# Another order of the SBUF allocations in a three-layer fp32 kernel on one core

## The chip, the core and the metric

One core of a Trainium2 chip runs the whole program. The core has five engines with a queue of instructions each: TensorE (PE; its weight loads are shown apart, as PEld), VectorE (DVE), ScalarE (ACT), GpSimd (POOL) and SyncE (SP), which issues the DMAs. The metric is the device time of one execution in microseconds. SBUF is the working memory; an address in it, here and below, is the byte offset within a partition.

## The reference

Two layers of a first block (normalisation, a mixer, normalisation, a feed-forward part with a convolution along the sequence), then one layer of a second block with two kinds of attention and 32 experts. There are 256 tokens of width 1,024, all in fp32. Cut to its frame:

```python
def first_block(x, ...):
    h = x
    for i in range(DEPTH):                       # DEPTH = 2: mla_mixer, then diff_mixer
        a = rms_norm(h, norm_g[i, 0])
        ...
        h = h + rms_norm(a, norm_g[i, 1])
        f = conv_ffn(rms_norm(h, norm_g[i, 2]), ffn_w_up[i], ffn_conv_w[i], ffn_conv_b[i], ffn_w_down[i])
        h = h + rms_norm(f, norm_g[i, 3])
    return h

def hybrid_layer(x, ...):
    h = rms_norm_2(x, g_mix)
    ...
    mixed = jax.nn.sigmoid(ga) * (o_a @ w_proj_a) + jax.nn.sigmoid(gb) * (o_b @ w_proj_b)
    x = x + mixed @ w_out
    x = x + hier_moe(rms_norm_2(x, g_ffn), w_group, b_group, w_expert, b_expert, w1, w3, w2)
    return x

    # in hier_moe, for each expert:
        hid = jax.nn.silu(xb @ w1[e]) * (xb @ w3[e])
        return hid @ w2[e]
```

The feed-forward part has 2,816 hidden columns, each expert 512. Each token goes to two experts.

## The kernel before

**Dense layers, to about 877 us.** Weights come in pieces of up to 128 x 2,048 fp32. SyncE loads a piece into one of four places of raw, ScalarE copies it to fp32r as the high part (L1330), and GpSimd subtracts the two for the low part (L635); both parts lie in parts, four places with a high and a low half each. TensorE multiplies in fp32r, three products for each pair of tiles, high x high, high x low, low x high, at L683, L684 and L685 in the helper product(). The activations are split in the same way: xh and xl, and for the second operand of a feed-forward part hh and hl. There are two forms. by_feature loads 128 columns of weights from parts as the stationary operand and streams 256 tokens of xh or xl past them (256 columns). by_token loads 128 tokens from xh, xl, hh or hl as the stationary operand and streams parts past them (mostly 512 columns). In the profile's names the streamed operand stands ahead of the stationary one: bank<-xh,parts is the 256-column form, bank<-parts,hh the 512-column form. A feed-forward layer has 33 pieces, 22 for the way up and 11 for the way down; pieces 8 to 31 are in a loop that runs twice over 12. keep_clock (L712) repeats a product of xh with itself where TensorE would otherwise pause.

**Attention** works in fp32 on views of room, a scratch buffer of 46,592 bytes for each partition. The probabilities of the second block's attention lie in xn and gpost and are transposed at L1146, with the identity from cs as the streamed operand.

**Experts, from about 877 us.** The experts run in 16 pairs. Each of the six weight matrices of a pair is a DMA of 2 MB into one of eight slots, taken in turn: six slots are the sixths of ring (which lies over raw and parts), one is the end of room, one is xspare (which lies over xh and xl). SyncE issues them at L592 as slots come free. Matmuls at L1258 (w1 and w3) and L1286 (w2) stream the slots at 512 columns past activations in room, two experts side by side in 64 columns of the array each. L1201 gathers the tokens and L1231 adds the result of a pair, from hh and hl with selT as the stationary operand. At the end VectorE adds to h (L2283), GpSimd applies the gains (L658) and the output is stored from xn.

**Where buffers lie.** sb(name, shape) takes the next free address, rounded up to 32 bytes; a buffer opened in a with statement gives its room back at the end of it, which is how ring lies over raw and parts, and xspare over xh and xl. The order of the calls at the head of build() is thus the map of SBUF. All semaphores, queues and the order of work are written out by hand further on in build() and don't look at addresses.

Of the kernel before, what the change touches and what calls it, by code (L numbers as in the profile page):

```python
# [28 lines left out]
F32R = mybir.dt.float32r  # L29
# [5 lines left out]
P = 128  # L35
S = 256
NT = S // P
D = 1024
KT = D // P
# [25 lines left out]
HALF = 2048  # L65
# [159 lines left out]
def build(nc, A, cst, out):  # L225
    G, A_, BANK, TURNS, W = plan()
    ctx = ExitStack()
    with ctx:
        def sb(name, shape, dt=F32):
            return ctx.enter_context(nc.sbuf_tensor(name, shape, dt))  # L230
# [6 lines left out]
        with nc.sbuf_tensor("raw", [P, RING, PIECE], F32) as raw, \  # L237
                nc.sbuf_tensor("parts", [P, PARTS, 2, PIECE], F32R) as both:
            high, low = both[:, :, 0, :], both[:, :, 1, :]
        ring = sb("ring", [P, 3 * RING, HALF])  # L240
        cs = sb("cs", [P, C_END + 5 * P + 16 * FT])
        prow = cs[:, C_END:C_END + 5 * P].rearrange("p (a b) -> p a b", b=P)
        subT = sb("subT", [P, 1])
        convT = cs[:, C_END + 5 * P:].rearrange("p (l w a j) -> p l w a j", l=2, w=4, a=2)
        gpre, gpost = sb("gpre", [P, D]), sb("gpost", [P, D])
        wr = sb("wr", [P, KT, NG + NE])
        br = sb("br", [P, NG + NE])
        lamp = sb("lamp", [P, 4, HD])
        h = sb("h", [P, NT, D])
        xn = sb("xn", [P, NT, D])  # L250
        with nc.sbuf_tensor("xh", [P, KT, S], F32R) as xh, nc.sbuf_tensor("xl", [P, KT, S], F32R) as xl:
            pass
        xspare = sb("xspare", [P, 2 * HALF])
        hh, hl = sb("hh", [P, 4, S], F32R), sb("hl", [P, 4, S], F32R)
        st = sb("st", [P, 64])
        eps_t = sb("eps_t", [P, 9])
        att = sb("att", [P, 4, 2, 2, 2])
        room = sb("room", [P, 11648])

        def view(at, n):  # L260
            return room[:, at:at + n]

        def r3(ap, **k):
            return ap.rearrange("p (a b) -> p a b", **k)
# [31 lines left out]
        qbT, kbT = r3(view(2048, 1024), b=S), r3(view(3072, 1024), b=S)  # L296
        va, vb = r3(view(6144, 1024), b=512), r3(view(7168, 1024), b=512)
        qiT, kiT = qrT, krT
        score = sb("score", [P, NT, S])
        selm = r3(prow[:, 0:4, :].rearrange("p a b -> p (a b)"), b=S)  # L300
        work = [score[:, :, :], selm]
        tanh_of = [view(4096, 2048), view(0, 2048)]
# [8 lines left out]
        silu = view(1536, EF)  # L311
        hidT = r3(view(2048, EF), b=P)
        Sel = view(2560, NT * 2 * CAP).rearrange("p (t e c) -> p t e c", t=NT, e=2)
        selT = sb("selT", [P, 2, NT, P], F32R)
        yh, yl = (y[:, :, :].rearrange("p a b -> p (a b)") for y in (hh, hl))
        gate, posm, mask = (r3(view(10240 + 64 * n, NT * NE), b=NE) for n in range(3))
        lg = r3(view(10432, NT * 36), b=36)
# [2037 lines left out]
```

## Time and profile before

| | us |
|---|---|
| median of three timed runs | 1345.78 |
| lowest and highest of them | 1342.06, 1347.07 |
| the profiled execution | 1344.84 |
| its span, first to last instruction | 1343.0 |

In the span TensorE is busy for 1282.2 us, GpSimd 573.2, ScalarE 548.2 and VectorE 509.6. The mean granted clock of TensorE is 0.994 of 2.4 GHz. The DMA moves 341.22 MB.

A matmul's time in the profile runs from its start to the modelled end of its way through the array, and the next one starts before that end. The pace of a run of products is therefore the distance between starts, which the view in order of time shows, and not the mean duration. Busy times of a group count overlapped time once.

### The profile page before, as it was taken

Reading aid. Unit: us, or ns where it says so; the run is one execution under the profiler, and the core shown is the slowest. Engines: PE = TensorE matmul, PEld = TensorE weight load, DVE = VectorE, ACT = ScalarE, POOL = GpSimd, SP = SyncE. Lnnn points to the kernel's source line nnn. Section 1 sums busy time; section 2 is a strip of 40 time slices with the busy share of each in tenths; the row PEclk is TensorE's granted clock in tenths of the full one; section 3 lists DMA queues with packets and bytes.
Section 4 is the critical chain, followed back from the end, with each engine's and each line's share of the span. In section 5 each row is a group of like instructions: output and inputs, shape, how many; then the busy total and the mean of one; then the engine's idle time right before and its main releaser. Section 6 shows DMA issues by size and latency. Waiting matters only on the chain.

```text
span 1343.0 us, 20033 instructions
## 1 busy us (share of the span) xinstructions
PE 1282.2 (95%) x7959; PEld 953.8 (71%) x7959; DVE 509.6 (38%) x1303; ACT 548.2 (41%) x853; POOL 573.2 (43%) x136
## 2 busy tenths in 40 slices
PE   6998999999998899999999999999999999999996
PEld 6867999998986799999878888854444444454442
DVE  2434444445265454444657453421111111111112
ACT  4654555556477465555543664311111111111112
POOL 4722788885944188888567855200000000000001
PEclk9999999999999999999999999999999999999998
DMA  7731566664633276664446544889999999999994
GB/s 270 235 94 63 184 194 188 188 193 151 220 126 95 63 205 195 196 188 165 150 164 204 158 137 161 335 342 405 427 428 427 429 429 429 429 428 428 428 424 185
DMA packets 157078, 341.22 MB, mean 254 GB/s; under 512 B 8554, under 2 KB 119499, under 8 KB 144331
## 3 DMA queue, kind: packets, MB, share of 16 engines
q1 hardware_dynamic: 157002, 340.18, 68.2%
q8 instruction: 53, 0.87, 0.3%
q14 instruction: 23, 0.18, 0.0%
HBM read 339.10 MB, written 1.05 MB: 253 GB/s over the span
## 4 chain that ended last, share of the span: by engine, by line
PE 77%; DMA 11%; ACT 4%; DVE 4%; POOL 2%; issue 1%; SPq 0%; ACTq 0%; DVEq 0%
PE bank L683 16%; PE bank L685 15%; PE bank L684 15%; PE bank L1258 12%; DMA ring<-in_w 6%; PE bank L1286 6%; DMA xspare<-in_w 4%; PE bank L1201 3%; PE bank L782 2%; POOL parts L635 2%; PE bank L693 1%; PE bank L1231 1%; ACT parts L1330 1%; PE bank L1119 1%; PE bank L1135 1%
## 5 line engine op out<-in xcount | busy, mean ns | idle before, releaser
L635 POOL TENSOR_TENSOR parts<-raw,parts 128x2048 fp32r<-128x2048 f32 (+4 forms) x128 | 568.0, 4464 | 289.8 <-ACT parts L1330 289.8
L683 PE MATMUL bank<-xh,parts 128*128 128x256 f32 x1032 | 288.0, 279 | 5.8 <-POOL parts L635 3.8
L684 PE MATMUL bank<-xl,parts 128*128 128x256 f32 x1032 | 285.8, 277 | 0.0
L685 PE MATMUL bank<-xh,parts 128*128 128x256 f32 x1032 | 285.8, 277 | 0.0
L1330 ACT ACTIVATE parts<-raw 128x2048 fp32r<-128x2048 f32 (+4 forms) x128 | 236.0, 1852 | 23.4 <-PE bank L683 8.5
L1258 PE MATMUL bank<-ring,room 128*64 128x512 f32 x768 | 226.1, 594 | 7.2 <-DMA ring<-in_w 5.3
L658 POOL TENSOR_TENSOR xn<-h,gpost 128x512 f32<-128x512 f32 x4 | 4.9, 1268 | 474.6 <-DVE h L2283 474.6
L683 PEld LDWEIGHTS bank<-xh,parts 128*128 128x128 f32 x1032 | 193.8, 188 | 12.4 <-issue 4.7
L684 PEld LDWEIGHTS bank<-xl,parts 128*128 128x128 f32 x1032 | 194.0, 188 | 0.8
L685 PEld LDWEIGHTS bank<-xh,parts 128*128 128x128 f32 x1032 | 194.0, 188 | 0.0
L1258 PEld LDWEIGHTS bank<-ring,room 128*64 128x64 f32 x768 | 72.6, 137 | 111.7 <-issue 111.7
L683 PE MATMUL bank<-parts,xh 128*128 128x512 f32 (+5 forms) x304 | 114.7, 377 | 5.9 <-DVE xl L1763 2.2
L1286 PE MATMUL bank<-ring,room 128*64 128x512 f32 x384 | 115.0, 600 | 0.7 <-ACT room L1693 0.7
L684 PE MATMUL bank<-parts,xh 128*128 128x512 f32 (+5 forms) x304 | 112.5, 370 | 0.0
L685 PE MATMUL bank<-parts,xl 128*128 128x512 f32 (+5 forms) x304 | 112.2, 369 | 0.0
L1693 ACT ACTIVATE room<-bank 128x512 f32<-128x512 f32 x16 | 9.6, 598 | 194.4 <-PE bank L1272 194.4
L685 PE MATMUL bank<-parts,hl 128*128 128x512 f32 x192 | 75.6, 394 | 0.0
L683 PE MATMUL bank<-parts,hh 128*128 128x512 f32 x192 | 74.8, 389 | 0.8 <-POOL parts L635 0.8
L684 PE MATMUL bank<-parts,hh 128*128 128x512 f32 x192 | 75.3, 392 | 0.0
L1509 ACT ACTIVATE room<-bank,room 128x256 f32<-128x256 f32 x64 | 32.7, 562 | 102.2 <-PE bank L685 101.0
L1367 ACT ACTIVATE room<-bank 128x512 f32<-128x512 f32 (+1 forms) x75 | 41.1, 581 | 75.1 <-PE bank L693 32.5
L1286 PEld LDWEIGHTS bank<-ring,room 128*64 128x64 f32 x384 | 34.9, 138 | 51.5 <-issue 49.3
(256 smaller groups left out, 1858.5 us busy)
## 6 DMA issues: line engine op xcount, KB each, us to landing
ring<-in_w SPq DMA_DIRECT2D x67, 2048.0 KB, 22.6
raw<-in_ffn_w_up SPq DMA_DIRECT2D x88, 512.0 KB, 4.9
raw<-in_ffn_w_down SPq DMA_DIRECT2D x44, 512.0 KB, 3.9
room<-in_w SPq DMA_DIRECT2D x11, 2048.0 KB, 19.9
xspare<-in_w SPq DMA_DIRECT2D x11, 2048.0 KB, 25.6
raw<-in_w_in SPq DMA_DIRECT2D x40, 512.0 KB, 4.0
raw<-in_diff_w_qkv SPq DMA_DIRECT2D x24, 512.0 KB, 4.6
ring<-in_w SPq DMA_DIRECT2D x10, 1024.0 KB, 25.0
```

What stands on the lines that cost most here:

```text
L635: pool.tensor_tensor(low[:, p % PARTS, 0:n], raw[:, p % RING, 0:n], high[:, p % PARTS, 0:n], ALU.subtract).then_inc(low_ready, 1)
L683: first = pe.matmul(out_, a[0], b[0], start=start, stop=False)
L684: pe.matmul(out_, a[0], b[1], start=False, stop=False)
L685: return first, pe.matmul(out_, a[1], b[0], start=False, stop=stop)
L693: ins = pe.transpose(b[0:cols, at:at + rows], src, ident[0:rows, 0:rows])
L782: ins = pe.matmul(b[:, t * S:t * S + S], qs[n][:, t * P:t * P + P], ks[n], start=n == 0, stop=n == len(qs) - 1)
L1201: ins = pe.matmul(bank[2 + k // 4][:, P * (k % 4):P * (k % 4) + P], xn[:, t, P * k:P * k + P], Sel[:, t].rearrange("p e c -> p (e c)"), st ...
L1258: ins = pe.matmul(bank[x][CAP * e:CAP * e + CAP, :], XgT[:, k, CAP * e:CAP * e + CAP], rows, start=k == 0, stop=k == KT - 1)
L1286: ins = pe.matmul(bank[1 + hf][CAP * e:CAP * e + CAP, :], hidT[:, k, CAP * e:CAP * e + CAP], rows_of(j, 2, e, k, D)[:, 512 * hf:512 * hf + ...
L1330: act.activation(high[:, p % PARTS, 0:n], raw[:, p % RING, 0:n], ACT.Copy).then_inc(high_ready, 1)
L1367: act.activation(dst, src, func, scale=scale).then_inc(bank_moved[BANK[g]], 1)
L1509: act.activation(fbuf[b][a], bank[b][:, a * S:a * S + S], ACT.Identity, bias=par(3, a), scale=par(1, a)).then_inc(centre, 1)
```

## The change

The calls that allocate the buffers stand in another order. The buffers that TensorE reads come first, each with a size that is a multiple of 512 bytes; the table of constants cs and the small columns (subT, wr, br, lamp, st, eps_t, att) come after them. Nothing else differs: on each of the five engines the built program has the same instructions in the same order (4,910 rows on PE, counting runs of equal ones once), with other addresses in them.

```diff
         ring = sb("ring", [P, 3 * RING, HALF])
+
+        with nc.sbuf_tensor("xh", [P, KT, S], F32R) as xh, nc.sbuf_tensor("xl", [P, KT, S], F32R) as xl:
+            pass
+        xspare = sb("xspare", [P, 2 * HALF])
+        hh, hl = sb("hh", [P, 4, S], F32R), sb("hl", [P, 4, S], F32R)
+        h = sb("h", [P, NT, D])
+        xn = sb("xn", [P, NT, D])
+        room = sb("room", [P, 11648])
+        gpre, gpost = sb("gpre", [P, D]), sb("gpost", [P, D])
+        score = sb("score", [P, NT, S])
+        selT = sb("selT", [P, 2, NT, P], F32R)
         cs = sb("cs", [P, C_END + 5 * P + 16 * FT])
         prow = cs[:, C_END:C_END + 5 * P].rearrange("p (a b) -> p a b", b=P)
         subT = sb("subT", [P, 1])
         convT = cs[:, C_END + 5 * P:].rearrange("p (l w a j) -> p l w a j", l=2, w=4, a=2)
-        gpre, gpost = sb("gpre", [P, D]), sb("gpost", [P, D])
         wr = sb("wr", [P, KT, NG + NE])
         br = sb("br", [P, NG + NE])
         lamp = sb("lamp", [P, 4, HD])
-        h = sb("h", [P, NT, D])
-        xn = sb("xn", [P, NT, D])
-        with nc.sbuf_tensor("xh", [P, KT, S], F32R) as xh, nc.sbuf_tensor("xl", [P, KT, S], F32R) as xl:
-            pass
-        xspare = sb("xspare", [P, 2 * HALF])
-        hh, hl = sb("hh", [P, 4, S], F32R), sb("hl", [P, 4, S], F32R)
         st = sb("st", [P, 64])
         eps_t = sb("eps_t", [P, 9])
         att = sb("att", [P, 4, 2, 2, 2])
-        room = sb("room", [P, 11648])
...
-        score = sb("score", [P, NT, S])
...
-        selT = sb("selT", [P, 2, NT, P], F32R)
```

The addresses that follow, from the built programs (bytes within a partition; "past" is the remainder after division by 512). The first 16,384 bytes are reserved and a few constants follow them, so that the first buffer starts at 16,512.

| buffer | bytes | before | past | after | past |
|---|---|---|---|---|---|
| raw, ring | 32,768, 98,304 | 16,512 | 128 | 16,512 | 128 |
| parts | 65,536 | 49,280 | 128 | 49,280 | 128 |
| xh, xspare | 8,192, 16,384 | 152,640 | 64 | 114,816 | 128 |
| xl | 8,192 | 160,832 | 64 | 123,008 | 128 |
| hh | 4,096 | 169,024 | 64 | 131,200 | 128 |
| hl | 4,096 | 173,120 | 64 | 135,296 | 128 |
| h | 8,192 | 136,256 | 64 | 139,392 | 128 |
| xn | 8,192 | 144,448 | 64 | 147,584 | 128 |
| room | 46,592 | 177,664 | 0 | 155,776 | 128 |
| gpre | 4,096 | 125,728 | 288 | 202,368 | 128 |
| gpost | 4,096 | 129,824 | 288 | 206,464 | 128 |
| score | 2,048 | 224,256 | 0 | 210,560 | 128 |
| selT | 2,048 | 226,304 | 0 | 212,608 | 128 |
| cs | 10,880 | 114,816 | 128 | 214,656 | 128 |
| wr | 1,152 | 133,920 | 288 | 225,568 | 288 |

## Rows read from the trace of the kernel before

**Rows 1.** The chain that ended last, by engine, and its shares by line.
```profile
PE 77%; DMA 11%; ACT 4%; DVE 4%; POOL 2%; issue 1%; SPq 0%; ACTq 0%; DVEq 0%
...
by line: PE bank L683 15.9%; PE bank L685 15.5%; PE bank L684 15.4%; PE bank L1258 11.7%; DMA ring<-in_w 6.1%; PE bank L1286 5.9%; DMA xspare<-in_w 4.5%; PE bank L1201 3.1%; PE bank L782 1.9%; POOL parts L635 1.5%; PE bank L693 1.4%; issue 
```

**Rows 2.** Stretches: us, each engine's busy us (instructions), PEclk, DMA share, GB/s.
```profile
180.00:304.00 124.00, 124.00 (x923) 117.11 (x923) 55.72 (x134) 66.67 (x82) 103.19 (x24) 1.00 0.64 197
464.00:476.00 12.00, 11.51 (x96) 11.30 (x96) 3.23 (x7) 6.04 (x7) 3.21 (x1) 1.00 0.01 1
...
1130.00:1290.00 160.00, 151.09 (x814) 73.96 (x812) 26.66 (x61) 18.96 (x26) 0.00 (x0) 1.00 1.01 429
```

**Rows 3.** Groups by line and shape, TensorE: count, busy us, mean ns, idle before.
```profile
L683 PE MATMUL bank<-xh,parts 128*128 128x256 f32 x1032 | 288.0, 279 | 5.8 <-POOL parts L635 3.8 <-issue 1.8 <-DVE room L1851 0.2
...
L683 PE MATMUL bank<-parts,xh 128*128 128x512 f32 x216 | 87.5, 405 | 3.2 <-DVE xl L1763 2.2 <-DVE xl L1761 1.0
...
L683 PE MATMUL bank<-parts,hh 128*128 128x512 f32 x192 | 74.8, 389 | 0.8 <-POOL parts L635 0.8
...
L683 PE MATMUL bank<-hh,parts 128*128 128x256 f32 x32 | 9.2, 286 | 0.0
```

**Rows 4.** In order of time, TensorE: start us, duration us, line, tiles, shape.
```profile
135.01 0.28 PE L683 MATMUL bank<-xh,parts 128*128 128x256 f32 x1
...
137.01 0.28 PE L685 MATMUL bank<-xh,parts 128*128 128x256 f32 x1
...
199.73 0.28 PE L685 MATMUL bank<-xh,parts 128*128 128x256 f32 x1
...
205.96 0.28 PE L683 MATMUL bank<-xh,parts 128*128 128x256 f32 x1
...
639.69 0.39 PE L684 MATMUL bank<-parts,hh 128*128 128x512 f32 x1
...
646.79 0.39 PE L685 MATMUL bank<-parts,hl 128*128 128x512 f32 x1
647.02 7.45 PE L712 MATMUL bank<-xh 128*128 128x512 f32 x32
```

**Rows 5.** Instructions of single tiles, TensorE: ns min/median/max, first and last start.
```profile
L1258 PE MATMUL bank<-xspare,room x128: 592/592/644, 906.8 to 1291.3; 128*64 128x512 f32 x128
...
L1258 PE MATMUL bank<-ring,room x720: 592/592/644, 906.8 to 1318.9; 128*64 128x512 f32 x180
...
L1258 PE MATMUL bank<-room x104: 592/592/643, 916.2 to 1261.9; 128*64 128x512 f32 x104
...
L1146 PE MATMUL bank<-cs,gpost x16: 272/273/328, 786.3 to 813.4; 128*128 128x128 f32 x16
...
L1146 PE MATMUL bank<-cs,xn x48: 271/273/329, 768.8 to 824.0; 128*128 128x128 f32 x48
```

**Rows 6.** VectorE and GpSimd: operations on gpost and gpre, and one on hh.
```profile
L1809 DVE TENSOR_TENSOR xn<-bank,gpost x16: 691/692/693, 117.4 to 647.9; 128x512 f32<-128x512 f32 x16
...
L658 POOL TENSOR_TENSOR xn<-h,gpost x4: 1264/1266/1277, 1332.9 to 1336.6; 128x512 f32<-128x512 f32 x4
...
L2192 DVE TENSOR_TENSOR xn<-h,gpre x4: 1079/1122/1226, 863.3 to 867.9; 128x512 f32<-128x512 f32 x4
...
L2275 DVE TENSOR_TENSOR hl<-bank,hh 128x512 fp32r<-128x512 f32 x32 | 22.1, 692 | 104.6 <-ACT hh L1696 104.6
```

**Rows 7.** The chain in order of time, experts' stage: start us, us, what.
```profile
899.92 7.02 PE bank L1286 x32
...
927.47 7.02 PE bank L1286 x32
...
1129.03 27.42 DMA ring<-in_w
1158.33 27.43 DMA ring<-in_w
1187.35 27.73 DMA ring<-in_w
```

## Prediction

> **What bounds the kernel now.** I read three views in this order: the page's busy shares with the chain of waits, the table of stretches, and the order of time inside the stretches. The first says that TensorE holds 77% of the chain and the DMA 11%, and that the fp32r products at L683 to L685 alone are 46.8% of it [rows 1]. The second splits the span in two halves. In the loop of a feed-forward stage TensorE has no gap at all, 124.00 of 124.00 us between 180 and 304 us, while GpSimd, the next engine, is busy 103.19 of them [rows 2]; the second such stage (464 to 647 us) has the same loop. A nanosecond more or less for each product there goes into the time one for one. In the later part of the experts' stage, 1130 to 1290 us, the DMA engines are busy for the whole stretch (share 1.01) at 429 GB/s and TensorE works only 151.09 of 160.00 us [rows 2]; there the end is set by the rate at which 2 MB weight tiles land. So an edit of addresses can act in two ways that count: through the pace of the products before 877 us, and through the rate of the transfers after it.
>
> **The change, part by part.** No instruction is added, removed or moved; all five engines issue the same rows in the same order. What changes is where each buffer starts, so every term is a number of instructions that read or write a moved buffer, times what its new start may do to one of them. First what the addresses become (table in the section on the change). The sizes of the moved buffers are multiples of 512 bytes, but what stands ahead of them (16,384 reserved bytes and the small constants) ends at 16,512, which is 128 past a multiple. So after the change no buffer that TensorE reads starts at a multiple of 512: ring, raw and parts stay where they are, at 128 past; xh, xl, xspare, hh, hl, h and xn go from 64 past to 128 past; room, score and selT, which do start at a multiple of 512 now, go to 128 past; gpre and gpost go from 288 past to 128 past. Every start is a multiple of 32 bytes in both kernels.
>
> (a) fp32 products of the experts' stage, stream side. The trace of before already has this instruction with its moving operand at three starts: xspare (64 past a multiple of 512), ring (128 past) and room (0 past). All three have a minimum and a median of 592 ns [rows 5]. And the 32 products that read only ring take 7.02 us in a row [rows 7]. Price: 0 ns each. Even if it weren't, the DMA covers it: a pair of experts takes TensorE 899.92 to 927.47, that is 27.55 us, against 29.31 us for its six transfers (below), so the products could be 6% slower before the end moved.
>
> (b) The weight side. The transposes at L1146 load their stationary operand from gpost (288 past) in 16 cases and from xn (64 past) in 48: both median 273 ns [rows 5]. Price: 0.
>
> (c) fp32r products, L683 to L685: 3 x 1,032 with 256 columns and xh or xl moving, 3 x 32 more with hh or hl (3,192 in all), and 3 x (216 + 192) = 1,224 with 512 columns and parts moving [rows 3]. This is the term that could matter, since they are the feed-forward stages. Their starts follow each other at more than one pace. At 200 us it is 6.23 us for 55 steps, 113.3 ns; at 135 us it is 2.00 us for 17 steps, 117.6 ns [rows 4]. Both stretches read the same xh, xl at the same addresses, and parts at starts equal modulo 512, so a pace that differs by 4.4 ns between them is no function of the address. I count 534 instructions at the slow pace (18 each at 33, 51 and 58 us, 192 from 132 us, 96 from 464 us, 48 each at 377, 763, 813 and 824 us). Nor is it the DMA: the slow stretch from 464 to 476 us has 11.51 us for 96 products and a DMA share of 0.01 [rows 2]. What selects the pace I can't read; it holds for a whole piece of weights and changes where a new run of products begins, so it looks like the rhythm in which loads and products interlock. With 512 columns it is 7.10 us for 31 steps, 229.0 ns, where weights come from hh, hl and the stream from parts; the 32 repetitions at L712, weights and stream both from xh, take 7.45 us, less 0.39 for the last one, over 31 steps: 227.7 ns [rows 4]. No row shows these forms with both operands at the same remainder, which is what they will have (both 128 past), except L712 (both 64 past). Bounds from those rows: all at the quick pace, 534 x 4.4 ns = 2.3 us and 1,224 x 1.3 ns = 1.6 us, so 3.9 us less; all at the slow pace, 2,658 x 4.4 = 11.7 us and, with the same 4.4 ns, 1,224 x 4.4 = 5.4 us, so 17.1 us more. I take 0, because rows at one address show both paces in the mix that stands.
>
> (d) VectorE, ScalarE, GpSimd. gpost is read by 16 operations of 691 to 693 ns at 288 past, and L2275, which reads hh, 64 past, has a mean of 692 for the same size [rows 6]. Price 0. The one form with a spread is L2192, a gather with stride on gpre, 1,079 to 1,226 ns x 4 [rows 6]: bound 4 x 0.15 = 0.6 us either way, and it lies on the path. The last four GpSimd operations are 1,264 to 1,277 ns [rows 6]; they stand beside other work of the tail and change by no more than their spread.
>
> (e) Transfers. Those into xspare and room have a new remainder, two of eight slots. Chain rows give landings at 1129.03 + 27.42 = 1156.45, 1158.33 + 27.43 = 1185.76 and 1187.35 + 27.73 = 1215.08 us [rows 7]. Between them are six transfers each, one into xspare, one into room and four into ring: 29.31 and 29.32 us, 4.89 us for 2 MB, which is the same 429 GB/s as the whole stage. Three remainders share one steady rate, so I take 0; if each transfer into a moved slot (two of eight, some 25 in all) were 1% off, 25 x 0.049 = 1.2 us either way.
>
> **The sum.** 0 + 0 + 0 + 0 + 0 against the profiled execution's own 1344.84 us (span 1343.0). The median of the three timed runs, 1345.78, is 0.9 higher, so the forecast is 1345.8 us.
>
> **A rule weighed.** The SBUF access that rows don't show is the fp32r stream at a new start. The Trainium skill, "SBUF — State Buffer", Specifications, says that lines are 16 bytes and that full bandwidth asks for two hits on a line. Every start here is a multiple of 32 before and after, so by that rule the change is worth exactly 0; the equal 592 ns of the three starts agree. Against it, "TensorE: Matmul & The Clock Gate", Back-to-back issue gap, gives N / 2.4 + 2.5 ns for a single warm product: 109.2 ns at 256 columns and 215.8 at 512, where this trace has 113.3 and 229.0. Something here costs 4.1 and 13.2 ns over that figure. If it were the starts, the estimate by that page is 3,192 x 4.1 + 1,224 x 13.2 ns + 2.3 us = 31.5 us, beside what the next part works out from rows.
>
> **Rivals.**
> *The quick pace everywhere* (0.08). With stationary and moving operand at the same remainder the interlock settles at the quick pace, as at L712. It gives 1345.8 - 3.9 = 1341.9 us, still within 0.5%. For it: L712 is the one row with equal remainders and is 1.3 ns quicker. Against it: L712 repeats one product, so nothing in it alternates.
> *The stream's overhead goes* (0.04). The quick pace is 113.3 ns for 256 columns at a granted clock of 1.00 (2.4 GHz), that is 272 cycles. If the 16 cycles above one for each column came from the starts at 64 past, 3,192 x 6.6 ns, the 2.3 us, and 1,224 x (229.0 - 213.3) ns go: 21.1 + 2.3 + 19.2 = 42.6 us, 1303.2 us. Against it: in the 512-column form the stream comes from parts, which is at 128 past already and stays there, and it has the overhead too [rows 4].
> *The slow pace everywhere* (0.05), the other side. Weights and stream at equal remainders meet in the same part of SBUF at each step, and the interlock settles at 117.6 ns in the feed-forward stages: 1345.8 + 17.1 = 1362.9 us. It decides from 6.7 us on, that is when about 1,500 more products run slow. For it: 534 do so already. Against it: all of those stand at the remainders of before, and so do the quick ones.
> *The change doesn't do what it says* is settled above: the starts are 128 past, not 0. What it adds is room and selT, which lose their multiple of 512. They feed the attention and the experts' stage; (a) shows room at 0 past no quicker than ring at 128 past, so it has the forecast's time and its chance is in it.
>
> **How the numbers follow.** Forecast 0.83 (1345.8 us, itself 1342 to 1349 by the spread of the three runs, 1342.06 to 1347.07, and the 1.8 us of (d) and (e)), quick pace 0.08, overhead gone 0.04, slow pace 0.05. What a measurement of this kernel can tell from no change is about 0.5%, 6.7 us. Faster by more: 0.04, plus 0.02 from a run of luck in the quick case: 0.06. Slower by more: 0.05, plus 0.01: 0.06. Same: 0.88. The range takes in the forecast's own bounds and the quick case and some hundred products that change pace the wrong way: 1339.5 to 1350.5.
>
> **What would show it.** In the profile of the changed kernel the order of time at 200 us should show 113.3 ns between starts, and 229.0 ns with 512 columns; a pace of 106.7 would prove the overhead case, 117.6 in the loops of the feed-forward stages the slow one. The three medians of L1258 should stay at 592, and the transfers at 4.89 us in 2 MB. If all these stand and the time has moved by more than 6.7 us, a wait has moved, and I am wrong about what an address can reach: the first place to look would be how often the slow pace occurs before 877 us.

## Result and the profile after

The changed kernel takes 1363.12 us (median of four runs, 1362.36 to 1364.86) against 1345.65 us in the same comparison: a ratio of 1.0124, 95% interval 1.0096 to 1.0153. It is slower by 17.5 us, outside the range, and on the side to which I had given 0.06.

First the page, its line on TensorE and the chain by line (the order of rows is as in [rows 1], with each line number one higher).

```profile
span 1360.6 us, 20033 instructions
PE 1300.1 (96%) x7959; PEld 972.7 (71%) x7959; DVE 510.1 (37%) x1303; ACT 547.7 (40%) x853; POOL 572.6 (42%) x136
...
PE 77%; DMA 11%; ACT 5%; DVE 4%; POOL 2%; issue 1%; SPq 0%; ACTq 0%; DVEq 0%
PE bank L684 16%; PE bank L685 15%; PE bank L686 15%; PE bank L1259 12%; DMA ring<-in_w 6%; PE bank L1287 6%; DMA xspare<-in_w 4%; PE bank L1202 3%; PE bank L783 2%; POOL parts L636 2%; PE bank L694 1%; PE bank L1232 1%; ACT parts L1331 1%; PE bank L1120 1%; PE bank L1136 1%
```

TensorE is busy 17.9 us longer with the same 7,959 matmuls, every other engine as long as before, within 0.6 us. The chain holds the same engines and lines with the same shares, within a point. The same stretch as in [rows 2], and the groups of [rows 3]:

```profile
180.00:304.00 124.00, 124.00 (x884) 117.25 (x884) 53.85 (x131) 62.48 (x77) 101.71 (x23) 1.00 0.62 189
```

```profile
L684 PE MATMUL bank<-xh,parts 128*128 128x256 f32 x1032 | 293.9, 285 | 5.6 <-POOL parts L636 3.6 <-issue 1.8 <-DVE room L1852 0.2
...
L684 PE MATMUL bank<-parts,xh 128*128 128x512 f32 x216 | 87.5, 405 | 3.2 <-DVE xl L1764 2.2 <-DVE xl L1762 1.0
...
L684 PE MATMUL bank<-parts,hh 128*128 128x512 f32 x192 | 75.0, 391 | 0.6 <-POOL parts L636 0.6
```

In the same 124 us without a gap there are 884 products and not 923. The form that has become clearly longer is 256 columns, xh or xl streamed past weights from parts, 285 ns for 279. (The last row has 391 ns for 389 although its pace, below, is the quicker one after the change: a mean duration doesn't tell the pace.) The order of time gives the distance between starts (columns as in [rows 4]).

```profile
199.67 0.28 PE L685 MATMUL bank<-xl,parts 128*128 128x256 f32 x1
...
205.91 0.28 PE L686 MATMUL bank<-xh,parts 128*128 128x256 f32 x1
...
653.30 0.39 PE L686 MATMUL bank<-parts,hl 128*128 128x512 f32 x1
...
658.74 0.39 PE L686 MATMUL bank<-parts,hl 128*128 128x512 f32 x1
```

With 256 columns it is 6.24 us for 52 steps, 120.0 ns, where [rows 4] gave 113.3 and 117.6. With 512 columns it is 5.44 us for 24 steps, 226.7 ns, a little quicker than the 229.0 of before. Over the whole trace (distances under 150 and 260 ns, so without waits) the means are:

| columns | before | after |
|---|---|---|
| 256, xh or xl streamed | 114.2 ns | 119.9 ns |
| 512, parts streamed | 229.2 ns | 227.7 ns |

3,192 x 5.7 - 1,224 x 1.5 ns = 16.4 us. That is nearly all of the 17.6 us between the spans. By stage, from the start of the first product in each:

| stage begins | before, us | after, us | grown in the stage ahead |
|---|---|---|---|
| first feed-forward | 132.46 | 132.43 | 0.0 |
| second layer's q, k, v | 328.01 | 333.30 | +5.3 |
| second feed-forward | 463.96 | 470.06 | +0.8 |
| keep_clock behind it | 647.02 | 658.97 | +5.9 |
| gates (256 columns again) | 750.87 | 765.53 | +2.7 |
| experts | 877.27 | 894.40 | +2.5 |
| end of the span | 1343.0 | 1360.6 | +0.5 |

The gains of 5.3, 5.9 and 2.5 us are where the 256-column form runs. The stage of q, k, v has 384 such products too; that it grew by 0.8 us alone goes with its mean granted clock, 0.97 before (328 to 464 us) and 0.99 after (333.3 to 470 us). The 2.7 us ahead of the gates are something else, a stretch of half clock that the first trace doesn't have there (rows further down).

Neither another engine nor a transfer is needed for the slower pace. In this stretch (columns as in [rows 2]) nothing but TensorE and its weight loads is at work, and the distances between starts are 120.0 ns there too:

```profile
134.00:137.00 3.00, 3.00 (x27) 3.00 (x27) 0.00 (x0) 0.00 (x0) 0.00 (x0) 1.00 0.00 0
```

What the experts' stage shows is as forecast:

```profile
L1259 PE MATMUL bank<-xspare,room x128: 592/592/643, 923.9 to 1308.9; 128*64 128x512 f32 x128
...
L1259 PE MATMUL bank<-ring,room x768: 592/592/644, 898.2 to 1336.4; 128*64 128x512 f32 x192
...
L1810 DVE TENSOR_TENSOR xn<-bank,gpost x16: 690/692/692, 117.4 to 659.9; 128x512 f32<-128x512 f32 x16
```

```profile
917.05 7.02 PE bank L1287 x32
...
1146.24 27.49 DMA ring<-in_w
1175.61 27.50 DMA ring<-in_w
1204.71 27.77 DMA ring<-in_w
```

fp32 products at 592 ns, with ring, xspare and room now all 128 past (as [rows 5], where they stood at three remainders), and a run of 32 at L1287 in 7.02 us in the chain (as [rows 7]), VectorE at 692 with gpost (as [rows 6]), and landings 29.38 and 29.37 us apart for six transfers, against 29.31 and 29.32 [rows 7].

### The profile page after: what moved, and what is told of

Its sections match the earlier page's. It is cut to its first block, busy times and chain, and to the rows that moved or that the text cites. A ratio compares the mean times of both kernels' runs of the same rounds, so it can differ in the third digit from the quotient of the medians.

```text
span 1360.6 us, 20033 instructions
## 1 busy us (share of the span) xinstructions
PE 1300.1 (96%) x7959; PEld 972.7 (71%) x7959; DVE 510.1 (37%) x1303; ACT 547.7 (40%) x853; POOL 572.6 (42%) x136
## 4 chain that ended last, share of the span: by engine, by line
PE 77%; DMA 11%; ACT 5%; DVE 4%; POOL 2%; issue 1%; SPq 0%; ACTq 0%; DVEq 0%
PE bank L684 16%; PE bank L685 15%; PE bank L686 15%; PE bank L1259 12%; DMA ring<-in_w 6%; PE bank L1287 6%; DMA xspare<-in_w 4%; PE bank L1202 3%; PE bank L783 2%; POOL parts L636 2%; PE bank L694 1%; PE bank L1232 1%; ACT parts L1331 1%; PE bank L1120 1%; PE bank L1136 1%
## 5 line engine op out<-in xcount | busy, mean ns | idle before, releaser
L684 PE MATMUL bank<-xh,parts 128*128 128x256 f32 x1032 | 293.9, 285 | 5.6 <-POOL parts L636 3.6
L685 PE MATMUL bank<-xl,parts 128*128 128x256 f32 x1032 | 291.9, 283 | 0.0
L686 PE MATMUL bank<-xh,parts 128*128 128x256 f32 x1032 | 291.9, 283 | 0.0
L684 PEld LDWEIGHTS bank<-xh,parts 128*128 128x128 f32 x1032 | 197.8, 192 | 12.1 <-issue 5.0
L685 PEld LDWEIGHTS bank<-xl,parts 128*128 128x128 f32 x1032 | 197.9, 192 | 0.7
L686 PEld LDWEIGHTS bank<-xh,parts 128*128 128x128 f32 x1032 | 197.9, 192 | 0.0
L1287 PE MATMUL bank<-ring,room 128*64 128x512 f32 x384 | 115.0, 600 | 0.7 <-ACT room L1694 0.7
L1510 ACT ACTIVATE room<-bank,room 128x256 f32<-128x256 f32 x64 | 32.6, 561 | 116.8 <-PE bank L686 116.8
L1287 PEld LDWEIGHTS bank<-ring,room 128*64 128x64 f32 x384 | 34.9, 138 | 51.6 <-issue 49.3
```

The lines of the kernel that those rows point to most:

```text
L684: first = pe.matmul(out_, a[0], b[0], start=start, stop=False)
L685: pe.matmul(out_, a[0], b[1], start=False, stop=False)
L686: return first, pe.matmul(out_, a[1], b[0], start=False, stop=stop)
L1287: ins = pe.matmul(bank[1 + hf][CAP * e:CAP * e + CAP, :], hidT[:, k, CAP * e:CAP * e + CAP], rows_of(j, 2, e, k, D)[:, 512 * hf:512 * hf + ...
L1510: act.activation(fbuf[b][a], bank[b][:, a * S:a * S + S], ACT.Identity, bias=par(3, a), scale=par(1, a)).then_inc(centre, 1)
```

## Experiments

All experiments put bytes of nothing (a buffer that no instruction touches) into the map of SBUF and change nothing else. I write d for xh's start minus parts' start, modulo 256 bytes. Each buffer of the x group (xh, xl, hh, hl) has the same d, unless said. The kernel before has d = 192 (64 less than parts' remainder), the changed one d = 0. Means are over distances between starts, as in the table above. Line numbers in the rows are shifted by the lines added.

**Is it the start of the x group, and against what?** The changed kernel with one line more:

```diff
         ring = sb("ring", [P, 3 * RING, HALF])
 
+        pad = sb("pad", [P, 16])
         with nc.sbuf_tensor("xh", [P, KT, S], F32R) as xh, nc.sbuf_tensor("xl", [P, KT, S], F32R) as xl:
```

> The changed kernel with 64 bytes of nothing ahead of xh, so that xh, xl, hh, hl and all that lies behind them start 192 past a multiple of 512, 64 off parts (128 past). Theory R (what counts is the remainder of the streamed operand's start against the stationary one's, parts): the 256-column form goes back from 120.0 to 113.3 ns between starts and the time to about 1346 us. Theory A (what counts is the remainder of xh's own start at 128 bytes or less): 192 is 64 past a multiple of 128 as before the change, so also about 1346 us; the next kernel parts the two. Theory M (the coarse distance, xh lying exactly 65,536 bytes behind parts): 113.3 ns too. Rival O (the order of the allocations, that is which buffer neighbours which, or the move of room, score, selT): 120.0 ns and 1363 us stay.

Measured: 1361.52 us, ratio 1.0115 (1.0082 to 1.0148). I had expected 1346 by three theories of four, and all three were wrong in that form. But the paces had changed: 117.5 ns with 256 columns (between 114.2 and 119.9) and 233.3 with 512 (above both). In order of time:

```profile
213.89 0.28 PE L685 MATMUL bank<-xh,parts 128*128 128x256 f32 x1
...
224.84 0.28 PE L685 MATMUL bank<-xh,parts 128*128 128x256 f32 x1
```

93 steps in 10.95 us, 117.7 ns. So the addresses change the paces with the order left as it is (whether the order has a share too, the run in the old order settles), and 64 bytes to one side (d = 64) do not give the average of 64 to the other (d = 192).

The same trace holds more than its average. The first two pieces of each feed-forward stage are a run of 192 products; the first 96 of the first stage go at the quick pace of the kernel before:

```profile
133.10 0.28 PE L686 MATMUL bank<-xl,parts 128*128 128x256 f32 x1
...
143.75 0.28 PE L687 MATMUL bank<-xh,parts 128*128 128x256 f32 x1
```

94 steps in 10.65 us, 113.3 ns, where the kernel before has 117.8 in its first 96. So d = 64 and d = 192 have the same two paces with 256 columns, in another mix: distances of 115 ns or less are 172 of the 3,192 here and 2,516 in the kernel before.

**Both operands moved together.** The same line ahead of raw:

```diff
+        pad = sb("pad", [P, 16])
         with nc.sbuf_tensor("raw", [P, RING, PIECE], F32) as raw, \
```

> The changed kernel with 64 bytes of nothing ahead of raw, so that every buffer that TensorE reads starts at 192 past a multiple of 512: xh and parts have equal remainders as in the changed kernel, but both are 64 past a multiple of 128. Theory R (relative): 120.0 ns stays and the time is about 1363 us. Theory A (absolute start of xh): 113.3 ns, 1346 us. Theory M (coarse distance 65,536, unchanged): 1363 us as R.

Measured: 1364.48 us, ratio 1.0133 (1.0106 to 1.0159), 119.9 and 227.7 ns: the changed kernel's paces to the tenth, though xh starts 64 bytes further than there and at the very address that it has in the run above.

```profile
215.32 0.28 PE L685 MATMUL bank<-xh,parts 128*128 128x256 f32 x1
...
226.48 0.28 PE L685 MATMUL bank<-xh,parts 128*128 128x256 f32 x1
```

93 steps in 11.16 us, 120.0 ns. xh at one address (114,880) gives 117.7 or 120.0 ns, depending on where parts lies. That speaks for the difference and against xh's own start.

**The slow form in the old order.** The kernel before with the line ahead of cs, which brings the x group to d = 0:

```diff
+        pad = sb("pad", [P, 16])
         cs = sb("cs", [P, C_END + 5 * P + 16 * FT])
```

> The kernel before, old order, with 64 bytes of nothing ahead of cs: xh, xl, hh, hl start 128 past, like parts, but lie 103,424 bytes behind parts (1,024 past a multiple of 2,048) and not 65,536. Theory R: the slow form comes without the change's order, 120.0 ns and about 1363 us. Theory M (only a distance that is a multiple of a large power of two hurts): 113.3 to 117.8 ns, 1346 us. Rival O (order or room): 1346 us, since the order is the old one.

Measured: 1363.74 us, ratio 1.0121 (1.0094 to 1.0148), 119.9 and 227.7 ns. The whole loss comes from 64 bytes, without the change. The coarse distance (theory M) is out: it is 103,424 bytes here and 65,536 in the changed kernel.

**room back at a multiple of 512.** The changed kernel with 384 bytes ahead of room:

> The changed kernel with 384 bytes of nothing ahead of room, so that room (and gpre, gpost, score, selT behind it) start at a multiple of 512, as room, score and selT do in the kernel before, while xh to xn stay at 128 past. Theories R, A, M: nothing to do with room, 120.0 ns and 1363 us stay. Rival O (room's loss of its multiple of 512 is the cost): back to about 1346 us.

Measured: 1363.11 us in one run, 119.9 and 227.7 ns. room, score, selT, gpre and gpost have no part in the loss.

**The period.** The changed kernel with 448, 192, 256 and 32 bytes ahead of xh (pad in the place of the first experiment, with another size).

> The changed kernel with 448 bytes of nothing ahead of xh: xh to xn start 64 past a multiple of 512, as before the change, but in the new order and 65,984 bytes behind parts. Theory R with a period of 512 bytes or less (what counts is xh's start minus parts' start, modulo 512; it was 448, that is -64, in the kernel before): the mix of before, 113.3 and 117.8 ns in the 256-column form, about 229 ns in the 512-column form, about 1346 us. If the period is longer than 512 or there is none: another pace, most likely a slow one (117.8 or 120.0 ns), 1360 us or more.

Measured: 1344.56 us, ratio 0.9995 (0.9982 to 1.0008). The new order with the old difference is as quick as the kernel before.

> 192 bytes of nothing ahead of xh: xh starts 192 bytes past parts' remainder, which is -64 modulo 256. Period 256: as the kernel before, 113.3 to 117.8 ns and about 1346 us. Period 512: a pace of its own; the start is 320 bytes off the good one, so I expect 117.8 to 120.0 ns, 1360 us.

Measured: 1345.04 us. I had expected about 1360; the period is 256, not 512.

> 256 bytes of nothing ahead of xh: difference of the remainders 256. If the conflict repeats every 256 bytes: 120.0 ns as in the changed kernel, 1363 us. If the period is 512, this is as far from the bad 0 as it can be: 113.3 ns or less (106.7 would be one column a cycle), 1346 us or down to about 1325 us.

Measured: 1363.15 us, 119.9 ns, as the changed kernel, which says the same.

> 32 bytes of nothing ahead of xh: between the measured 0 (120.0 ns, 227.7 ns with 512 columns) and +64 (117.5 and 233.3 ns). If the pace goes in steps of 64 bytes it equals one of the two; if it goes in finer steps, the 256-column form is between them, near 119 ns; about 1362 us either way.

Measured: 1364.49 us, 116.8 and 233.3 ns.

**The rest of the circle.** 128, 160, 224 and 96 bytes.

> 128 bytes of nothing ahead of xh: difference of the starts 128 modulo 256, the middle between the two bad sides seen so far (0: 120.0 ns, 64: 117.5 ns) and next to the good one (192: 114.4 ns). Theory R with period 256, with a pace that follows the distance from 0: 113.3 ns or less in the 256-column form, 1346 us or less. Rival, a one-sided rule (only the last 64 bytes before parts' remainder are good, since a stationary load that starts ahead of the stream keeps ahead of it): 117.5 ns and about 1360 us.

Measured: 1362.46 us, ratio 1.0118 (1.007 to 1.0165), 118.7 ns. The distance theory is wrong: half way round is no better.

> Difference 160, between 128 and the good 192. By the distance theory about 113.3 to 114.4 ns, 1343 to 1346 us; by the one-sided rule a mix, near 116 ns and 1353 us. Steps of 32 bytes showed a pace of their own at 32 (116.8 ns, between four values), so a mix of several distances between starts is expected here too.

> Difference 224, that is -32, between the good 192 and the bad 256 (0). By the distance theory as bad as +32: about 116.8 ns with 256 columns and 233 ns with 512, 1364 us. By the one-sided rule still good: 114 ns, 1346 us.

> Difference 96, between 64 (117.5 ns, 233.3 ns) and 128. By the distance theory about 115 ns and 1352 us or less; by the one-sided rule 117 ns and 1360 us.

Measured: 1364.28, 1366.18 and 1371.12 us. Neither theory holds: d = 224 and d = 160, the neighbours of the good one at 32 bytes, both are slow, and 96 is the worst of all. Together, with what the paces are worth against the kernel before, 3,192 x the difference at 256 columns and 1,224 x that at 512:

| d, bytes | 256 columns, ns | 512 columns, ns | worth, us | span less 1343.0, us |
|---|---|---|---|---|
| 192 (before) | 114.2 | 229.2 | 0 | 0 |
| 192 (x_192) | 114.4 | 229.0 | +0.4 | +0.2 |
| 192 (x_448) | 114.3 | 229.0 | +0.1 | +0.8 |
| 224 | 118.3 | 233.3 | +18.1 | +21.4 |
| 0 (changed kernel) | 119.9 | 227.7 | +16.4 | +17.6 |
| 32 | 116.8 | 233.3 | +13.3 | +19.7 |
| 64 | 117.5 | 233.3 | +15.6 | +16.8 |
| 96 | 119.9 | 234.0 | +24.1 | +26.2 |
| 128 | 118.7 | 232.4 | +18.3 | +18.0 |
| 160 | 118.0 | 233.2 | +17.0 | +19.5 |

The paces give the size of each loss but not the exact order of the spans: by the paces d = 128 costs more than 160 and 224, and its span is shorter than both. d = 32 is furthest off, and its trace has more half clock than any other:

```profile
core 0: 1362.7 us, clock 0.987
```

against 0.994 before. For the others the worth lies within 3.3 us of the span's growth. (The kernel before itself took from 1342.06 to 1354.59 us over all its timed runs.) Of eight values in steps of 32 bytes one has a quick average, as long as all x buffers share it, and the kernel before had it.

**The difference or the streamed start: parts moved alone.** What all runs but one had left open. Against x_256 (slow), where xh starts at 115,072 too, only parts moves, by 64 bytes:

```diff
-        with nc.sbuf_tensor("raw", [P, RING, PIECE], F32) as raw, \
+        with nc.sbuf_tensor("raw", [P, RING, PIECE], F32) as raw, nc.sbuf_tensor("gap", [P, 16], F32), \
                 nc.sbuf_tensor("parts", [P, PARTS, 2, PIECE], F32R) as both:
...
+        pad = sb("pad", [P, 64])
         with nc.sbuf_tensor("xh", [P, KT, S], F32R) as xh, nc.sbuf_tensor("xl", [P, KT, S], F32R) as xl:
```

> The kernel of the run x_256 (slow, 1363 us; xh and all behind it 128 past a multiple of 256) with 64 bytes of nothing between raw and parts, so that parts alone moves, to 192 past; xh's start minus parts' start is then -64, that is 192 modulo 256. Theory R: the pace is that of the kernel before and of x_192, about 114.3 ns with 256 columns and 229 ns with 512, and about 1346 us, although every x buffer stands where the slow kernel has it. Rival (the streamed operand's own start counts, and parts' doesn't): 119.9 ns and 1363 us.

Measured: 1346.30 us, ratio 1.0005 (0.9983 to 1.0028), 114.4 and 229.0 ns.

```profile
213.30 0.28 PE L685 MATMUL bank<-xh,parts 128*128 128x256 f32 x1
...
223.86 0.28 PE L685 MATMUL bank<-xh,parts 128*128 128x256 f32 x1
```

93 steps in 10.56 us, 113.5 ns. With every x buffer where the slow kernel has it, moving the weights by 64 bytes gives the 17 us back. It is the difference that counts, and not the start of either operand.

**One of three products.** x_192 with xl alone 64 bytes further (d = 0 for xl, 192 for xh, hh and hl; hh, hl and what follows are moved by 256 bytes, which keeps d).

> The quick kernel x_192 with xl alone 64 bytes further, so that xh is at difference 192 and xl at 0; hh, hl keep 192. Of three products two stream xh and one xl. If each product's pace comes from its own streamed tile against the weights loaded beside it: the distances after L683 and L685 products stay near 113.3 ns and the one for xl goes to 120.0, mean 115.5 ns, about 1350 us. If the slowest of the three sets the rhythm: 120 ns for all, 1363 us.

Measured: 1360.09 us in one run, 118.4 ns on average. In the loop of the first feed-forward stage the distances after the three products are 117.3, 119.7 and 116.4 ns, the middle one after the product that streams xl, 117.8 on average. In the loop of the second they are 120.8, 118.9 and 117.9. So there is no pace of 113.3 left for the products that stream xh, and with one buffer at another difference the products that stream the other buffer are slower too. Neither theory had that.

**hh and hl alone.** x_192 with hh, hl and what lies behind them 64 bytes further.

> The quick kernel x_192 with hh, hl and what lies behind them 64 bytes further: hh, hl at difference 0, xh, xl at 192. Theory R, buffer by buffer: 512-column products that load hh, hl go from 229.0 to 227.7 ns (576 of them, 0.7 us less), the 96 that stream hh, hl from 115.8 to 119.8 ns (0.4 us more), those with xh, xl stay at 114.4 and 229.1; the time stays at 1345 us.

Measured: 1354.23 us in one run, where I had expected 1345. The 512-column products that load hh and hl do go to 226.8 ns. But the 256-column products, none of whose operands has moved, go from 114.4 to 116.5 ns:

```profile
213.72 0.28 PE L686 MATMUL bank<-xh,parts 128*128 128x256 f32 x1
...
224.67 0.28 PE L686 MATMUL bank<-xh,parts 128*128 128x256 f32 x1
```

93 steps in 10.95 us, 117.7 ns, where x_192 has 113.3 in the same piece. At d = 192 both paces are steady, and which one a piece gets is not set by its own operands: of the 3,192 products, those at 115 ns or less number 2,516 in the kernel before, 2,399 in x_192 and 915 here. In the loops hh and hl are the only moved buffers that TensorE reads, in the products just ahead of each piece; h, xn, room and what follows moved too, so that it was hh and hl is likely and not shown. It also means that an average of 114.4 ns needs more than d = 192 for xh and xl. Each count is from one trace.

## Why the prediction was wrong

**What bounds the kernel** held. TensorE has no gap in the feed-forward loops, a longer product goes into the time one for one, and the experts' stage only moved: it begins 17.1 us later and ends 17.6 us later.

**Terms (a), (b), (d) and (e)** held at 0: 592 ns with all slots at 128 past, 692 ns with gpost, transposes at L1147 (L1146 before) with a median of 273 ns in both traces, 4.90 us for 2 MB against 4.89. That room, score and selT lost their multiple of 512 cost nothing, by the run room_0.

**Term (c) is the step that failed.** It said that "a pace that differs by 4.4 ns between them is no function of the address", because [rows 4] shows two paces at equal remainders. The observation was right and the inference wrong. Which steady paces there are goes with the difference of the starts (at d = 192 and d = 64: 113.3 and 117.7; at d = 0: 120.0 alone), and which of two a piece gets goes with something outside its own operands, as hh_0 shows. I took two values at one address for proof that the address has no say, when I had rows at one difference only. The term was 0 in my sum and measures 16.4 us.

**The slow rival** is the case that came: forecast 1362.9 us at a chance of 0.05, measured 1363.12. It was right that the products slow down when the two operands come to equal remainders. But equal remainders are not what sets a slow kernel apart: the six other differences tried, besides 192, cost 15 us or more as well. That the two reads meet in the same part of SBUF is not shown. The size is luck to a good part: I had 2,658 products at +4.4 ns and 5.4 us for the 512-column form; in truth all 3,192 go to 120.0 ns, a pace that no row of before has, and the 512-column form becomes 1.5 ns quicker. The argument against it, that slow and quick products stand at the same remainders, was the wrong step again. Its price came near the cost by two errors that cancel, and the range left it out by that argument.

**The quick rival** had taken L712, both operands in xh, as its evidence for equal remainders. For 512 columns it was a good guide (226.7 to 227.7 ns, as the changed kernel has), for 256 columns it said nothing.

**The overhead rival** falls: 113.3 ns for 256 columns is the best pace of any run.

**The rules weighed.** The Trainium skill, "SBUF — State Buffer", Specifications, with its 16-byte lines, was read in the prediction as putting the change at exactly 0. The measurement decides against reading it so: the pace of products whose loads and streams overlap changes here over steps of 32 bytes and repeats after 256. Whether the rule holds for one access by itself, no run here shows. The estimate from the Trainium skill, "TensorE: Matmul & The Clock Gate", Back-to-back issue gap, 109.2 ns for 256 columns by its formula for a single warm product, is reached by no steady run of fp32r products here, and the 31.5 us that the prediction estimated from it, had the change taken the whole distance to that figure away, did not come.

**A second, smaller effect** is the clock. In the stretch after the second feed-forward stage:

```profile
712.00:724.00 12.00, 12.00 (x42) 9.20 (x40) 11.62 (x22) 5.27 (x5) 7.67 (x2) 0.74 0.17 48
```

against the same work before:

```profile
700.00:712.00 12.00, 12.00 (x55) 9.58 (x53) 11.62 (x27) 5.87 (x6) 8.45 (x2) 1.00 0.23 79
```

42 matmuls and not 55 at a granted clock of 0.74: a spell at the lower level (1.2 GHz), which makes up the 2.7 us of the stage table. In the 12 us ahead of it TensorE was busy for 10.75 us, and for 10.74 in the kernel before, whose clock did not fall. Such spells come and go between kernels of one pace (x_192 has none there) and between executions of one kernel: the mean granted clock of the kernel before goes from 0.986 (1354.59 us) to 0.996 (1342.11 us) over its timed runs. I can't say what called this one up; that the products alone are worth 16.4 of 17.6 us says that it is not the main cause.

**Open.** What in the hardware makes the pace depend on the difference, with a period of 256 bytes and only one quick average among eight, isn't shown. That the load of the next weights and the stream of the running product ask for the same part of SBUF at the same moment would fit, but it was only argued. What picks one of the two paces at d = 192 and d = 64 is open too, and with it whether d = 64 could be as quick as 192 in another map of the buffers. No version that I ran beats the kernel before: the best have its difference and its time.

## What to carry to other kernels

Two buffers that TensorE reads side by side, one as the stationary and one as the streamed operand of fp32r products, have a difference of starts that was worth up to 5% of a product's pace here (114.2 to 119.9 ns). "Aligned" is no virtue in it: here equal remainders are among the bad ones, and 64 bytes of nothing between two buffers cost 1.2% of the whole time (old_order_rel0). So after any edit of the map of SBUF, compare the distance between starts for each form of product with that of before, even when no instruction changed. And where a trace shows two values of a quantity under one setting, it has not shown that the setting doesn't matter.

## What was not expected of the hardware

- The pace of fp32r products with 128 x 128 weights and 256 columns takes steady values of 113.3 and 117.7 (d = 192 and 64) and 120.0 ns (d = 0), all at a granted clock of 1.00; at the other differences single distances, most of them between 112 and 125 ns, repeat in a mix. With 512 columns the averages go from 226.7 to 234.0 ns.
- The average depends on the difference of the two operands' starts modulo 256 bytes, in steps as fine as 32 bytes, and not on either start alone (all_64, parts_64). The 120.0 ns stand with every other engine and the DMA idle (134 to 137 us after the change).
- fp32 products (592 ns at 512 columns and 128 x 64 weights) show none of it in the cases met here: the start of ring less that of room goes from 128 to 0 modulo 256 with the change, and 32 of them take 7.02 us before and after.
- With the same addresses of its own operands, a run of products can keep 113.3 or 117.7 ns through nearly a whole piece of 96, and moving only other buffers can turn one into the other (x_192 against hh_0, 9.2 us in single runs).
